# The late residual stream kept by tokens instead of by features

## The chip, the cores and the metric

One NeuronCore of a Trainium2 chip runs the whole program. The metric is device time in microseconds, the median of several executions. The engines are TensorE (PE, with PEld for its weight loads), VectorE (DVE), ScalarE (ACT), GpSimd (POOL) and the DMA queues, of which SyncE (SP) issues the hardware ones.

## The reference, cut to what matters

256 tokens of width D = 1024 pass through two blocks. The first (two layers of attention, pooling and a sparse expert network) is not changed. The second has six residual updates, each of this form, with ALPHA = sqrt(2):

```python
def layer_norm(x, g, b):
    mu = jnp.mean(xf, axis=-1, keepdims=True)
    var = jnp.mean(jnp.square(xf - mu), axis=-1, keepdims=True)
    return ((xf - mu) * lax.rsqrt(var + LN_EPS)).astype(x.dtype) * g + b
...
def post_norm_update(x, y, gate, res_w, g, b):
    return layer_norm(DN_ALPHA * x + res_w * gate * y, g, b)
```

y is the output of a sublayer on `x * (1 + scale) + shift`: a SwiGLU network (1024 to 2 x 2816 to 1024; res_w 0.5), a neighbourhood attention with an output projection, or a three-tap convolution with input and output projections (res_w 1). gate, shift and scale are rows of width D computed from the condition vector. The order of the second block is ffn.0.0, attention (qkv, na_o), ffn.0.1, ffn.1.0, convolution (conv_in, conv_o), ffn.1.1. The five updates behind na_o, ffn.0.1, ffn.1.0, conv_o and ffn.1.1 are called boundaries 0 to 4 here; behind boundary 4 the result is the output.

## The kernel before

Everything streams through one weight stream. SP loads units of 128 x 1024 fp32 (512 KB) into a ring of four `raw` tiles. ACT splits each half of a unit (128 x 512) into a high part `wh` (L677, `hi`), DVE makes the low part `wl` (L1135, `lo`), and PE does three products for each pair of operands (high x high, high x low, low x high). wh and wl are rings of four halves, so ACT and DVE run at most two units ahead of PE, and each half is given back by PE through `halves_free`. The order of instructions on each engine is written out by hand; semaphores join them. Some units are "folds": DVE multiplies 128 x 1024 weights by a condition vector and sums (L1159), which gives one column of the modulation table `mod2`.

The activations lie by features: `X` is 128 partitions (features within a tile) x 8 tiles (k) x 256 tokens. A norm statistic is therefore a sum over partitions, which PE makes with a matrix of 1/D (`column_mean`, L2219), the result being spread over all partitions.

`pairs` is a SwiGLU stage: 22 rounds of two input units (gate and up projection, PE L2032 to L2035, operand stationary weights) and one output unit. The output unit is applied by `token_rows`: tokens are the stationary side, so its sum lies by tokens in banks 0 to 3 (two token tiles x two halves of 512 features). na_o and conv_o are `product` stages instead (PE L2010 to L2012): a unit gives one output feature tile, and DVE adds it to X at once with the gate as a column (`residual`, L1206). One unit needs all eight operand tiles.

What happens at a boundary behind a SwiGLU stage, in order: PE drains (`finish_acc`); ACT and DVE copy the four banks to `token_sums` (L834, L1344); PE turns them by 16 transposes (`turn_sum`, L2210); DVE adds each feature tile to X (`stream_sum`, L1349); PE sums for the mean (L2219); DVE subtracts it (`centre`, L1767); ACT squares (L813); PE sums again (L2219); ACT takes the root (L817); DVE inverts 128 x 256 values (`invert`, L1318); then for each of the eight tiles DVE scales (L1305), ACT writes the high part XH with the shift (L806), DVE the low part XL (L1296), and PE does the first two units of the next stage tile by tile as XH and XL come (`merged_opening`, L2032). Behind na_o and conv_o the order is the same from the mean on.

The residual base of the next boundary, ALPHA * (g * normed + b), is made in X during the next stage: DVE multiplies (`update_view`, L1773), POOL adds the bias column (L659). Behind boundary 4 DVE multiplies by the inverse (L1996), ACT applies g and b (L1112) and SP stores X in four DMAs (L588).

In the conv_in stage DVE also does the convolution (`convolve`, five operations on each tile), and conv_o opens when all eight operand tiles are there. `keep_busy` is PE work without a use, between sums and opening.

Of the kernel before, what the change touches and what calls it, by code (L numbers as in the profile page):

```python
# [113 lines left out]
def plan():  # L114
# [32 lines left out]
    add("na_o", KT, True, KT)  # L147
# [3 lines left out]
    add("conv_o", KT, True, KT)  # L151
# [60 lines left out]

def column_places():
    at, out = 0, {}
    for name, n in COLUMNS:
        out[name] = (at, n)
        at += n
    return out, at
# [37 lines left out]
def build(nc, ctx, stream, columns, tables, x_in, ctx_in, rpb, c_rows, h_spill, c_spill, out):  # L256
# [61 lines left out]
    UNREAD = 62  # L318
    banks = [ctx.enter_context(nc.psum_tensor(f"bank{i}", [P, 512], F32)) for i in range(8)]
# [38 lines left out]
    CONV, CU, CT = 16384, 2048, 4352  # L358

# [26 lines left out]


# [54 lines left out]
    acc_done = sem("acc_done")  # L442
# [29 lines left out]
    view_coef_ready = sem("view_coef_ready")  # L472

# [26 lines left out]


    @block.sync
    def _(sp):
# [82 lines left out]
        for k in range(0, KT, 2):  # L586
            sp.wait_ge(x_done, KT * DEPTH + k + 2)
            sp.dma_start(out[:, k:k + 2, :], X[:, k:k + 2, :]).then_inc(stored, 16)  # L588
        sp.wait_ge(stored, 16 * KT // 2)
# [3 lines left out]
    def _(pool):  # L593
# [60 lines left out]
        for n, name in enumerate(("ffn.0.0.x", "qkv", "ffn.0.1", "ffn.1.0", "conv_in", "ffn.1.1")):  # L654
            pool.wait_ge(xl_ready, made[name])
            pool.wait_ge(view_coef_ready, n + 1)
            for k in range(KT):
                pool.wait_ge(view_step, KT * n + k + 1)
                pool.tensor_scalar(X[:, k, :], X[:, k, :], view_coef[:, 1, k:k + 1], None, ALU.add)\  # L659
                    .then_inc(view_ready, 1)  # L660


    @block.scalar
    def _(act):
# [165 lines left out]
        def copy_sum():  # L830

            act.wait_ge(acc_done, seen("acc_done"))
            for half in range(2):
                act.activation(token_sums[:, 0, HALF * half:HALF * (half + 1)], banks[half][:, :],  # L834
# [10 lines left out]
        for l in range(DEPTH):  # L845
# [139 lines left out]
            if l == 0:  # L985
                copy_sum()
# [16 lines left out]
        def layer_norm(updates, func=ACT.Silu):  # L1003
            seen("stat_ready")
            take_table(ACT.Sqrt)
            squares(X, ZSQ, centred, "centred")
            token_root(banks[7], func, rms, updates)


        hooks = {-1: copy_sum, 0: lambda: squares(X, ZSQ, x_done, "x_done"),  # L1010
# [9 lines left out]
        hooks = {-1: copy_sum, 1: context_squares, 4: lambda: stream_root(banks[7][:, 0:T], 1)}  # L1020
# [16 lines left out]
        copy_sum()  # L1037
# [49 lines left out]
        head_pair_out(KT - 1)  # L1087
        product(stages["na_o"], then=stages["ffn.0.1"], both=True)
        layer_norm(2)
        operand(range(KT), modul, shift)  # L1090
        pairs(stages["ffn.0.1"], 2, ACT.Silu, then=stages["ffn.1.0"], opened=True)
        copy_sum()
        hi(stages["ffn.1.0"], 1)
        layer_norm(3)
        operand(range(KT), modul, shift)
        pairs(stages["ffn.1.0"], 2, ACT.Silu, then=stages["conv_in"], opened=True)
        copy_sum()
        hi(stages["conv_in"], 1)
        layer_norm(4)
        operand(range(KT), modul, shift)  # L1100
        product(stages["conv_in"], to_arena(CONV), then=stages["conv_o"], opened=True)
        operand(range(KT), modul)
        product(stages["conv_o"], then=stages["ffn.1.1"], both=True)
        layer_norm(5)
        operand(range(KT), modul, shift)
        pairs(stages["ffn.1.1"], 2, ACT.Silu, opened=True)
        copy_sum()
        layer_norm(6)

        for k in range(KT):  # L1110
            act.wait_ge(centred, seen("centred"))
            act.activation(X[:, k, :], X[:, k, :], ACT.Identity, bias=column("ln_b.1.2", k),  # L1112
                           scale=column("ln_g.1.2", k)).then_inc(x_done, 1)
# [3 lines left out]
    def _(dve):  # L1117
# [222 lines left out]
        def stream_sum(factor, view, semaphore):  # L1340

            dve.wait_ge(acc_done, seen("acc_done"))
            for half in range(2):
                dve.tensor_copy(token_sums[:, 1, HALF * half:HALF * (half + 1)], banks[2 + half][:, :])\  # L1344
# [34 lines left out]
        for l in range(DEPTH):  # L1379
# [362 lines left out]
            if l == 0:  # L1742
                stream_sum(lambda k: mod1[:, 0, 40 + k:41 + k], X_, x_done)
# [15 lines left out]
        def residual_factor(l, base, side, res):  # L1759
            step(dve.tensor_scalar(scale[:, :], modulation(l, base, 2, side), res, None, MUL))  # L1760
            settle()

# [19 lines left out]
        def last_experts():  # L1782
            stream_sum(lambda k: mod1[:, DEPTH - 1, 40 + k:41 + k], X_, x_done)
# [29 lines left out]
        def context_sum():  # L1813
            stream_sum(factor_of_sum, ctx_tiles, evacuated)
# [27 lines left out]
        stream_sum(factor_of_sum, X_, evacuated)  # L1842
# [4 lines left out]
        product(st, None, 3, 9)  # L1847
# [67 lines left out]
        dve.wait_ge(view_ready, 1 + 2 * KT)  # L1915
        add_bias(0, 2, 40, 48)
        add_bias(0, 2, 48, 72)
        residual_factor(0, 24, 0, 1.0)

        def coefficients(l, which, next_l, next_base):  # L1920

            name = (f"ln_g.{l}.{which}", f"ln_b.{l}.{which}")
            operand_coefficients(next_l, next_base, 0, *name)
            stream_coefficients(*name)

        def layer_norm(then):

            centre(X_)
            lo(then, 1)
            invert(rms)  # L1930
            operand(X_, modul, factor, shift, rms)

        def ffn(name, l, which, updates, then, after=None):

            def coefficients_after():
                if name == "ffn.1.1":
                    add_bias(1, 2, 64, 72)
                residual_factor(l, 0 if which == 0 else 48, 0, 0.5)
                if after is not None:
                    dve.wait_ge(view_ready, 1 + KT * updates)  # L1940
                    add_bias(1, 2, *((0, 24) if after == (1, 0) else (24, 40)))
                    coefficients(l, which, *after)
            hooks = {n + 1: lambda n=n: update_view((2 * n, 2 * n + 1)) for n in range(4)}
            hooks[8] = coefficients_after
# [765 lines left out]
```

## Time and profile before

| | |
|---|---|
| three runs | 3606.43, 3608.0, 3611.11 us; median 3608.0 us |
| profiled execution | span 3608.2 us |
| busy share | PE 97%, PEld 88%, DVE 79%, ACT 57%, POOL 6% |
| mean granted clock of PE | 0.994 of full speed |
| largest groups on DVE and ACT | wl 1453.1 us (2180 x 691 ns), wh 1318.5 us (2180 x 629 ns) |
| DMA | 788.31 MB, mean 218 GB/s |

The span is one execution from first to last instruction; it stands 0.2 us from the median of the runs. A busy PE is one whose pipeline holds something; whether it does useful work must be read from the lines it executes.

### The profile page before, as it was taken

Reading aid. Unit: us, or ns where it says so; the run is one execution under the profiler, and the core shown is the slowest. Engines: PE = TensorE matmul, PEld = TensorE weight load, DVE = VectorE, ACT = ScalarE, POOL = GpSimd, SP = SyncE. Lnnn points to the kernel's source line nnn. Section 1 sums busy time; section 2 is a strip of 40 time slices with the busy share of each in tenths; the row PEclk is TensorE's granted clock in tenths of the full one; section 3 lists DMA queues with packets and bytes.
Section 4 is the critical chain, followed back from the end, with each engine's and each line's share of the span. In section 5 each row is a group of like instructions: output and inputs, shape, how many; then the busy total and the mean of one; then the engine's idle time right before and its main releaser. Section 6 shows DMA issues by size and latency. Waiting matters only on the chain.

```text
span 3608.2 us, 66759 instructions
## 1 busy us (share of the span) xinstructions
PE 3492.3 (97%) x22828; PEld 3162.8 (88%) x22828; DVE 2866.3 (79%) x5956; ACT 2053.0 (57%) x4303; POOL 228.9 (6%) x341
## 2 busy tenths in 40 slices
PE   6999999999999999999999999999999999999998
PEld 6988999998888888999998888898987888889887
DVE  6876987767777778798968778688887788887776
ACT  4554558875555455457875556444454655555555
POOL 0000111110000000111110000010001010101000
PEclk8999999999999999999999999999999999999999
DMA  8556666667776657667757777776766177676463
GB/s 304 199 172 216 223 218 219 220 208 240 241 240 212 224 179 247 225 219 232 245 182 254 240 241 257 220 238 230 251 226 222 54 239 250 199 250 203 146 225 130
DMA packets 246521, 788.31 MB, mean 218 GB/s; under 512 B 30160, under 2 KB 62928, under 8 KB 246048
## 3 DMA queue, kind: packets, MB, share of 16 engines
q1 hardware_dynamic: 230544, 737.78, 63.3%
q0 software_dynamic: 15760, 47.78, 3.7%
q8 instruction: 120, 1.97, 0.2%
q14 instruction: 97, 0.79, 0.1%
HBM read 749.78 MB, written 35.65 MB: 218 GB/s over the span
## 4 chain that ended last, share of the span: by engine, by line
PE 72%; DVE 12%; PEld 7%; issue 4%; DMA 2%; ACT 2%; PEldq 1%; SPq 0%; ACTq 0%; DVEq 0%
PE bank L2010 11%; PE bank L2011 10%; PE bank L2012 10%; PE bank L2032 9%; PE bank L2125 6%; PE bank L2127 6%; PE bank L2126 6%; PE bank L2033 4%; DVE wl L1135 4%; PE bank L2379 3%; PEld bank L2125 2%; PEld bank L2127 2%; PEld bank L2126 2%; DMA raw<-stream 2%; PE bank L2219 2%
## 5 line engine op out<-in xcount | busy, mean ns | idle before, releaser
L1135 DVE TENSOR_TENSOR wl<-raw,wh 128x512 fp32r<-128x512 f32 x2180 | 1453.1, 691 | 462.7 <-ACT wh L677 454.9
L677 ACT ACTIVATE wh<-raw 128x512 fp32r<-128x512 f32 x2180 | 1318.5, 629 | 802.1 <-PE bank L2127 389.9
L2010 PE MATMUL bank<-XHL,wh 128*128 128x256 f32 x3424 | 992.8, 290 | 40.7 <-DVE wl L1135 25.8
L2011 PE MATMUL bank<-XHL,wh 128*128 128x256 f32 x3424 | 970.8, 284 | 0.0
L2012 PE MATMUL bank<-XHL,wl 128*128 128x256 f32 x3424 | 970.6, 283 | 0.0
L2010 PEld LDWEIGHTS bank<-XHL,wh 128*128 128x128 f32 x3424 | 658.3, 192 | 58.7 <-issue 31.8
L2011 PEld LDWEIGHTS bank<-XHL,wh 128*128 128x128 f32 x3424 | 659.1, 192 | 1.8 <-issue 1.0
L2012 PEld LDWEIGHTS bank<-XHL,wl 128*128 128x128 f32 x3424 | 658.3, 192 | 0.0
L2125 PE MATMUL bank<-wh,AH 128*128 128x512 f32 x1464 | 571.6, 390 | 3.7 <-DVE wl L1135 2.1
L2126 PE MATMUL bank<-wl,AH 128*128 128x512 f32 x1464 | 570.1, 389 | 0.0
L2127 PE MATMUL bank<-wh,AL 128*128 128x512 f32 x1464 | 569.6, 389 | 0.0
L2032 PE MATMUL bank<-XHL,wh 128*128 128x512 f32 x1372 | 494.1, 399 | 4.8 <-DVE XHL L1296 4.8
L2033 PE MATMUL bank<-XHL,wl 128*128 128x256 f32 x1372 | 384.9, 281 | 0.0
L2125 PEld LDWEIGHTS bank<-wh,AH 128*128 128x128 f32 x1464 | 275.0, 188 | 60.6 <-issue 2.8
L2127 PEld LDWEIGHTS bank<-wh,AL 128*128 128x128 f32 x1464 | 274.9, 188 | 57.6
L2126 PEld LDWEIGHTS bank<-wl,AH 128*128 128x128 f32 x1464 | 275.1, 188 | 56.2
L2032 PEld LDWEIGHTS bank<-XHL,wh 128*128 128x128 f32 x1372 | 258.1, 188 | 64.4 <-issue 6.7
L2033 PEld LDWEIGHTS bank<-XHL,wl 128*128 128x128 f32 x1372 | 259.2, 189 | 7.6
L959 ACT ACTIVATE side<-bank 128x256 f32<-128x256 f32 x256 | 98.1, 383 | 277.1 <-PE bank L2012 271.2
L631 POOL DMA_DIRECT2D h_spill<-side x256 | 138.4, 541 | 1000.4 <-ACT side L959 988.6
L953 ACT ACTIVATE side<-side,routed 128x128 f32<-128x128 f32 x512 | 163.0, 396 | 0.9
L1693 DVE TENSOR_TENSOR side<-side,arena 128x256 f32<-128x256 f32 x256 | 159.5, 623 | 0.1
(272 smaller groups left out, 4251.5 us busy)
## 6 DMA issues: line engine op xcount, KB each, us to landing
raw<-stream SPq DMA_DIRECT2D x1340, 512.0 KB, 4.4
h_spill<-side POOLq DMA_DIRECT2D x256, 128.0 KB, 3.4
side<-h_spill SPq DMA_DIRECT2D x256, 128.0 KB, 3.8
arena<-rpb POOLq DMA_DIRECT2D x4, 1024.0 KB, 28.9
arena<-tables POOLq DMA_DIRECT2D x2, 832.0 KB, 8.6
X<-x_t POOLq DMA_DIRECT2D x1, 1024.0 KB, 8.2
side<-c_rows POOLq DMA_DIRECT2D x2, 512.0 KB, 7.7
c_spill<-side POOLq DMA_DIRECT2D x2, 512.0 KB, 4.5
```

Of the source, the lines that this page charges most:

```text
L677: act.activation(wh[:, n % 4, :], raw[:, q % 4, HALF * half:HALF * (half + 1)], ACT.Copy).then_inc(hi_ready, 1)
L953: last = act.activation(by_weight[:, b % 2, n * P:(n + 1) * P], unweighted[:, n * P:(n + 1) * P], ACT.Copy, scale=routed[:, 2, t:t + 1])
L1135: tt_op(wl[:, n % 4, :], raw[:, q % 4, HALF * half:HALF * (half + 1)], wh[:, n % 4, :].bitcast(F32), SUB).then_inc(lo_ready, 1)
L1693: tt_op(AP_[:, j % 2, :].unsqueeze(2), HV[:, j % 4, :].unsqueeze(2), gates[:, :, bass.ds(j + more, 1)], MUL).then_inc(gate_done, 1)
L2010: pe.matmul(out, wh[:, n % 4, a:b], moving_h, start=start, stop=False, skip_group_check=check)
L2011: pe.matmul(out, wh[:, n % 4, a:b], moving_l, start=False, stop=False, skip_group_check=check)
L2012: return pe.matmul(out, wl[:, n % 4, a:b], moving_h, start=False, stop=stop, skip_group_check=check)
L2032: pe.matmul(out, wh[:, n % 4, a:b], both, start=kt == 0, stop=False, skip_group_check=True)
L2033: return pe.matmul(out[:, 0:T], wl[:, n % 4, a:b], high, start=False, stop=False, skip_group_check=True)
L2125: pe.matmul(out, high, wh[:, n % 4, :], start=first, stop=False)
L2126: pe.matmul(out, high, wl[:, n % 4, :], start=False, stop=False)
L2127: last = pe.matmul(out, low, wh[:, n % 4, :], start=False, stop=final)
```

## The change

X is read and written by tokens behind na_o (`XT`, the same memory as 128 tokens x 2 token tiles x 1024 features) and is never turned into features again except into the operand. Norm statistics become two columns (one value for each token of a tile), g, b and gate become rows of 1024 spread over all partitions: g and b by a broadcast DMA from a new input `norm_rows`, the gate by a DMA of its column to memory, a broadcast DMA back and a POOL copy that puts it in order. na_o and conv_o take weight rows like the SwiGLU output unit (`projection_rows`), with the unit k needing operand tile k alone. The base is made by POOL alone. The `stream_sum` of earlier stages waits for halves of the last unit instead of a drain. The store goes by tokens.

```diff
 @block.gpsimd
+        def load_gate(n):
+            pool.wait_ge(gate_column, n + 1)
+            pool.dma_start(gate_spill[n, :].rearrange("(p k) -> p k", k=KT), scale[:, :]).then_inc(gate_spilled, 16)
+            pool.wait_ge(gate_spilled, 16 * (n + 1))
+            pool.dma_start(A(GATE_SPREAD, D), gate_spill[n:n + 1, :].broadcast_to([P, D])).then_inc(gate_loaded, 16)
+            pool.wait_ge(gate_loaded, 16 * (n + 1))
+            pool.tensor_copy(A(GATE_ROW, D).rearrange("p (k w) -> p k w", w=P),
+                             A(GATE_SPREAD, D).rearrange("p (w k) -> p k w", k=KT)).then_inc(gate_ready, 1)
...
+        load_gate(0)
+        for n, name in enumerate(("ffn.0.1", "ffn.1.0", "conv_in", "ffn.1.1")):
+            pool.wait_ge(xl_ready, made[name])
+            load_norm(n)
+            pool.wait_ge(norms_loaded, 32 * (n + 1))
+            for tt in range(TT):
+                pool.tensor_tensor(XT[:, tt, :], XT[:, tt, :], A(NORM_ROWS[n], D), ALU.mult).then_inc(base_step, 1)
+            for tt in range(TT):
+                pool.wait_ge(base_step, TT * n + tt + 1)
+                pool.tensor_tensor(XT[:, tt, :], XT[:, tt, :], A(NORM_ROWS[n] + D, D), ALU.add).then_inc(base_ready, 1)
+            load_gate(n + 1)
+        load_norm(4)
 @block.scalar
+        def token_statistics(n):
+            for c in range(len(CHUNKS)):
+                act.wait_ge(local_mean, len(CHUNKS) * n + c + 1)
+                act.activation(A(SQUARED + HALF * c, HALF), tokens_of(c), ACT.Square, bias=stat(LOCAL + c),
+                               accum_out=stat(SPREAD + c)).then_inc(spread_ready, 1)
...
+        def boundary(n, func=ACT.Silu):
+            token_statistics(n)
+            act.wait_ge(inverse_ready, n + 1)
+            for half in range(2):
+                part = XT[:, 0, HALF * half:HALF * (half + 1)]
+                act.activation(part, part, ACT.Identity, bias=stat(OFFSET), scale=stat(INVERSE)).then_inc(normed_first, 1)
+            for k in range(KT):
+                act.wait_ge(moved_ready, KT * n + k + 1)
+                act.activation(XH[:, k, :], modul[:, k, :], ACT.Copy).then_inc(xh_ready, 1)
+            if func is not None:
+                take_table(func)
 @block.vector
+        def token_sums_closed(st, n):
...
+                step(tt_op(A(GATED + HALF * c, HALF), banks[2 * tt + half][:, :], gate_row(half), MUL))
...
+                step(dve.scalar_tensor_tensor(tokens_of(c), base, base_scale, A(GATED + HALF * c, HALF), MUL, ADD,
+                                              accum_out=stat(TOTAL + c)))
...
+            gated(0)
+            gated(1)
+            if n == 0:
+                dve.wait_ge(base_turned, 1)
+            added(0)
+            gated(2)
+            added(1)
+            mean(0)
+            gated(3)
+            added(2)
+            mean(1)
+            added(3)
+            mean(2)
+            mean(3)
...
+        def boundary(st, n, then):
+            token_sums_closed(st, n)
+            lo_half(then, 1, 0)
+            variance(n)
+            lo_half(then, 1, 1)
+            inverse(n)
+            tt_op(stat(OFFSET, 1), stat(MEAN, 1), stat(INVERSE, 1), MUL).then_inc(inverse_ready, 1)
+            for half in range(2):
+                part = XT[:, 1, HALF * half:HALF * (half + 1)]
+                dve.tensor_scalar(part, part, stat(MEAN + 1), stat(INVERSE + 1), ADD, MUL).then_inc(normed_second, 1)
...
+            def moved(k):
...
+                dve.tensor_scalar(modul[:, k, :], turned_tile(n, k), coef[:, 0, k:k + 1], coef[:, 1, k:k + 1], MUL,
+                                  ADD).then_inc(moved_ready, 1)
+            moved(0)
+            for k in range(KT):
+                if k + 1 < KT:
+                    moved(k + 1)
+                dve.wait_ge(moved_ready, KT * n + k + 1)
+                rest((k,), modul)
...
+        co = stages["conv_o"]
+        rest((0, 1), modul)
+        product(co, None, 0, 1)
         convolve(KT - 1)
+        rest((2,), modul)
+        for k in range(3, KT):
+            product(co, None, k - 2, k - 1)
+            rest((k,), modul)
         add_bias(1, 2, 40, 64)
+        gate_factor(1, 24, 1.0, 3)
 @block.tensor
-        def finish_acc():
-            pe.drain().then_inc(acc_done, 1)
+        def boundary(n):
+            pe.wait_ge(local_mean, len(CHUNKS) * n + 1)
+            keep_busy(18, banks[4])
+            for half in range(2):
+                pe.wait_ge(normed_first, 2 * n + half + 1)
+                pe.wait_ge(normed_second, 2 * n + half + 1)
...
+                        last = pe.transpose(turned_tile(n, o)[:, tt * P:(tt + 1) * P], XT[:, tt, o * P:(o + 1) * P],
+                                            ident[:, :])
...
+        projection_rows(stages["na_o"], 0, KT - 1)
...
+        for tt in range(TT):
+            for o in range(KT):
+                last = pe.transpose(banks[4 + 2 * tt + o // 4][:, (o % 4) * P:(o % 4 + 1) * P],
+                                    X[:, o, tt * P:(tt + 1) * P], ident[:, :])
+        last.then_inc(base_turned, 1)
+        projection_rows(stages["na_o"], KT - 1, KT)
+        boundary(0)
```

In `token_sums_closed`, gated(c) multiplies a bank of 128 x 512 by the gate row, added(c) adds it to the base with a running sum, and mean(c) makes the column of a chunk's mean; the four chunks are (tile 0, half 0), (tile 1, half 0), (tile 0, half 1), (tile 1, half 1). `token_rows` and `projection_rows` signal `first_tokens` behind the first token tile of each half of the last unit. Behind boundary 4, DVE does two `scalar_tensor_tensor` of 128 x 512 for each of the four chunks (centre and g; inverse and b), and SP stores each chunk (256 KB). In the SwiGLU stages `update_view` is gone from DVE, and the gate column is made in round 8 of 22; for boundary 3 it is made in conv_o, as shown.

## Rows read from the trace of the kernel before

**Rows 1.** Page, busy time of the engines.

```profile
PE 3492.3 (97%) x22828; PEld 3162.8 (88%) x22828; DVE 2866.3 (79%) x5956; ACT 2053.0 (57%) x4303; POOL 228.9 (6%) x341
```

**Rows 2.** Timeline, boundary 1: start, duration, engine, line, tiles, count [idle before].

```profile
3065.78 2.49 DVE L1135 TENSOR_TENSOR wl<-raw,wh 128x512 fp32r<-128x512 f32 x4
...
3066.61 0.47 PE L2125 MATMUL bank<-wh,AH 128*128 128x512 f32 x1 [0.29 <-DVE wl L1135]
...
3069.23 0.39 PE L2127 MATMUL bank<-wh,AL 128*128 128x512 f32 x1
...
3070.61 1.94 PE L2210 MATMUL bank<-ident,arena 128*128 128x128 f32 x16 [0.99 <-DVE arena L1344]
...
3081.29 1.75 DVE L1318 RECIPROCAL arena<-arena 128x256 f32<-128x256 f32 x1 [1.31 <-ACT arena L817]
...
3084.78 0.47 PE L2032 MATMUL bank<-XHL,wh 128*128 128x512 f32 x1 [0.96 <-DVE XHL L1296]
```

**Rows 3.** Timelines of PE and ACT, boundary 0.

```profile
2872.07 3.62 PE L2219 MATMUL bank<-X,mean_d 128*128 128x256 f32 x16
...
2884.46 0.47 PE L2032 MATMUL bank<-XHL,wh 128*128 128x512 f32 x1 [0.96 <-DVE XHL L1296]
...
2889.11 0.62 ACT L677 ACTIVATE wh<-raw 128x512 fp32r<-128x512 f32 x1
...
2890.63 0.44 PE L2032 MATMUL bank<-XHL,wh 128*128 128x512 f32 x1
```

**Rows 4.** Timeline, conv_o; windows (last: PE's clock, DMA share, GB/s).

```profile
3359.73 2.10 DVE L1294 TENSOR_TENSOR XHL<-arena,XHL 128x256 fp32r<-128x256 f32 x6
...
3389.75 0.48 DVE L1206 SCALAR_TENSOR_TENSOR X<-bank,scale,X 128x256 f32<-128x256 f32 x1 [1.20 <-PE bank L2012]
...
3401.93 0.47 PE L2032 MATMUL bank<-XHL,wh 128*128 128x512 f32 x1 [0.96 <-DVE XHL L1296]
...
3365.00:3370.00 5.00, 3.64 (x18) 3.43 (x18) 3.90 (x13) 1.57 (x4) 0.00 (x0) 0.55 0.28 93
```

**Rows 5.** Timeline of the end.

```profile
3583.31 1.29 DVE L1135 TENSOR_TENSOR wl<-raw,wh 128x512 fp32r<-128x512 f32 x2
...
3601.40 4.04 ACT L1112 ACTIVATE X<-X,cols 128x256 f32<-128x256 f32 x8 [0.77 <-DVE X L1996]
```

**Rows 6.** Groups by form behind 2600 us: busy, mean ns of one.

```profile
L1901 DVE TENSOR_SCALAR arena<-arena,small 128x512 f32<-128x512 f32 x32 | 14.1, 483 | 0.6
...
L1065 ACT ACTIVATE arena<-bank,small 128x512 f32<-128x512 f32 x32 | 21.7, 684 | 6.4 <-DVE small L1891 6.4
...
L821 ACT ACT_TABLE_LOAD x10 | 12.8, 1283 | 0.2
```

**Rows 7.** POOL's operations; DVE without and beside them; windows of ffn.0.1.

```profile
L659 POOL TENSOR_SCALAR X<-X,view_coef x48: 917/1565/1951, 2369.9 to 3449.2; 128x256 f32<-128x256 f32 x48
...
L653 POOL TENSOR_SCALAR arena<-arena 128x2048 f32<-128x2048 f32 x1 | 5.9, 5937 | 10.7 <-DMA arena<-tables 10.7
...
2361.48 2.63 DVE L1135 TENSOR_TENSOR wl<-raw,wh 128x512 fp32r<-128x512 f32 x4
...
2369.98 2.90 DVE L1135 TENSOR_TENSOR wl<-raw,wh 128x512 fp32r<-128x512 f32 x4
...
2900.00:3050.00 150.00, 150.00 (x791) 128.41 (x790) 127.13 (x250) 83.20 (x162) 9.96 (x8) 1.00 0.77 253
```

**Rows 8.** DMA issues (KB, us to landing); a wait in the chain.

```profile
h_spill<-side POOLq DMA_DIRECT2D x256, 128.0 KB, 3.4
...
arena<-rpb POOLq DMA_DIRECT2D x4, 1024.0 KB, 28.9
...
side<-c_rows POOLq DMA_DIRECT2D x2, 512.0 KB, 7.7
...
side<-c_spill POOLq DMA_DIRECT2D x2, 512.0 KB, 4.0
...
2258.63 15.26 DMA raw<-stream
```

More of the change, by code:

```diff
@@ L1036, in _ @@
         product(st, keep, 0, 1)
-        copy_sum()
+        copy_sum(stages["ffn.0.0.x"])
         product(st, keep, 1, 5)
@@ L1087, in _ @@
         head_pair_out(KT - 1)
+        take_table(ACT.Sqrt)
         product(stages["na_o"], then=stages["ffn.0.1"], both=True)
-        layer_norm(2)
-        operand(range(KT), modul, shift)
+        boundary(0)
         pairs(stages["ffn.0.1"], 2, ACT.Silu, then=stages["ffn.1.0"], opened=True)
-        copy_sum()
+        take_table(ACT.Sqrt)
         hi(stages["ffn.1.0"], 1)
-        layer_norm(3)
-        operand(range(KT), modul, shift)
+        boundary(1)
         pairs(stages["ffn.1.0"], 2, ACT.Silu, then=stages["conv_in"], opened=True)
-        copy_sum()
+        take_table(ACT.Sqrt)
         hi(stages["conv_in"], 1)
[L1099 to L1105, printed above, removed]
-        pairs(stages["ffn.1.1"], 2, ACT.Silu, opened=True)
[L1107 to L1113, printed above, removed]
+        boundary(2, None)
+        st = stages["conv_o"]
+        product(stages["conv_in"], to_arena(CONV), then=st, opened=True)
+        operand((0, 1), modul)
+        for k in range(2, KT):
+            product(st, None, k - 2, k - 1)
+            operand((k,), modul)
+        product(st, None, KT - 2, KT, then=stages["ffn.1.1"], both=True)
+        boundary(3)
+        pairs(stages["ffn.1.1"], 2, ACT.Silu, opened=True)
+        take_table(ACT.Sqrt)
+        token_statistics(4)
     @block.vector
@@ L1935, in coefficients_after, with ffn @@
+        def ffn(name, l, which, n, then, after=None):
             def coefficients_after():
@@ L2531, in _ @@
+        projection_rows(stages["na_o"], 0, KT - 1)
+        pe.wait_ge(view_ready, 1 + 2 * KT)
+        pe.wait_ge(xl_ready, made["na_o"])
+        for tt in range(TT):
+            for o in range(KT):
[3 more added lines that the diff above has]
+        projection_rows(stages["na_o"], KT - 1, KT)
+        boundary(0)
         pairs(stages["ffn.0.1"], 2, opened=True)
-        finish_acc()
@@ L2544, in _ @@
+        keep_busy(4, banks[0])
+        projection_rows(stages["conv_o"], 0, KT)
+        keep_busy(8, banks[4])
+        boundary(3)
         pairs(stages["ffn.1.1"], 2, opened=True)
-        finish_acc()
-        turn_sum()
-        stream_norm(evacuated, "evacuated")
 def shape_tables():
```

284 lines of the change are left out of this document (191 added, 93 removed).

## The prediction, written before the changed kernel was run

> **What bounds the kernel now.** The page comes first: PE is busy for 97% of the span [rows 1], so outside the boundaries the time is PE's and a saving on DVE or ACT is worth nothing. A timeline of each boundary comes next, because there PE's busy time is sums, `keep_busy` and waiting, and the order is a chain over DVE, ACT and PE. At boundary 1 the last wl is ready at 3065.78 + 2.49 = 3068.3 (two of these four belong to the next stage), the last matmul starts at 3069.23, and the first matmul of ffn.1.0 at 3084.78 [rows 2]: 15.5 us, boundary 2 alike. At boundary 0 it is 2872.07 to 2884.46, 12.4 us [rows 3]; at boundary 3 3389.75 to 3401.93, 12.2 us [rows 4]; behind the last wl at 3583.31 + 1.29 = 3584.6 the end takes 23.6 us [rows 5]. The reader is to see that five short stretches, some 80 us in all, hold all that this change can give, and that the rest can only be disturbed. Time is therefore summed boundary by boundary, as the shift of the first matmul behind each.
>
> **A boundary behind a SwiGLU stage (1 and 2).** Removed: the drain, copies, adding, two column means, the 1.75 us inversion of 128 x 256 [rows 2]. In their place: DVE can begin at 3068.3, when its wl are done, since the first token tile's bank closes half-way through PE's last six matmuls. A two-input operation of 128 x 512 has a pitch of 2.49 / 4 = 0.62 us [rows 2]; with its running sum 0.70 is taken (an estimate, one short accumulator read more). Four gated, four added, four short means of 0.12: 2.5 + 2.8 + 0.5 = 5.8, to 3074.1. ACT squares two chunks behind the last means, 0.68 each [rows 6]: 3075.5. Then column operations with a wait each (variance 0.2, root 0.3, inverse and offset 0.4) and half a lo in between, 1.3 in all: 3076.8. Normalising 128 x 512 costs DVE 0.48 [rows 6] and ACT about 0.7, which is the longer; first four transposes 0.5 (1.94 / 16 each [rows 2]), hand-overs 0.3, moved 0.35, ACT's copy 0.4, rest 0.35 (2.10 / 6 [rows 4]) and 0.2 to PE: 2.8, to 3079.6. Against 3084.78: **5.2 us**. At boundary 2 a fold of two pitches is behind the normalising, half of it open: **4.6**. Each of these sums is held good to 1.5 us.
>
> One work moves into the open. `take_table(Silu)` was hidden beside the inversion; now it stands behind the last XH, and a table load takes 1.28 us [rows 6]. Queued behind it on ACT is the high part of the third unit. Before, this was at 2889.11, and PE took that unit up at 2890.63, 6.2 us behind the opening's start [rows 3]. After it: opening paced at 0.72 for a tile (moved and rest), XH(7) at +4.45, table to +5.9, hi +6.5, lo +7.1, PE at +7.3. **Loss 1.1 us** at boundaries 0, 1 and 3; at boundary 2 there is no table load, and the faster pace gives 0.3.
>
> **Boundary 0.** Weight rows need 12 matmuls of 512 columns in place of 24 of 256; by the pitch (3069.23 - 3066.61) / 11 = 0.24 [rows 2], 0.23 in an unbroken run, a unit is 2.73 us against 24 x 0.12 = 2.88, 1.2 us for eight. Sixteen transposes for the base are put in front of the last unit, 1.94 us, and the table load before its second hi opens 0.4. The projection so ends 0.8 later, near 2872.9. DVE starts 1.9 before that (at 2871.0), needs 5.8 and then the same 1.4 + 1.3 + 2.8 = 5.5: 2882.3 against 2884.46, **2.1 us**; with the table 1.0.
>
> **Boundary 3.** Before, conv_o's first unit waited for all eight operand tiles, six of which DVE gave from 3359.7 on and two only behind the last convolution, and PE then ran part of it slowly: between 3365 and 3370 the granted clock is 0.55, partly at the 1.2 GHz level [rows 4], behind five microseconds in which PE was half idle. After it, unit 0 starts with tile 0, at 3360.1; each later unit's lo and rest come in time (unit 1 at 3362.8, unit 2 at 3365.6), so the projection ends at 3360.1 + 8 x 2.73 = 3382 against some 3389.6. DVE could start at 3380.5 and PE open at 3391.8, 10 us early. But the gate row is not there. Its column is made behind rest(7), which waits for lo(6), which waits for unit 4: 3360.1 + 5 x 2.73 + hi 0.6 + lo 0.65 + rest 0.35 + two column steps 0.4 = 3375.8, with a wait's play 3375.9. Behind it are a 4 KB write, a broadcast read of 512 KB and a POOL copy of 128 x 1024. The write: nothing so small is shown; 128 KB land in 3.4, so 3.0 is taken (bounds 2.0 and 3.4). The read: 4.0 to 7.7 for 512 KB, 4.6 taken as nearest to those of one DMA alone [rows 8]. The copy: 5.94 / 2 = 3.0 by the large POOL operation, up to 1.95 x 4 = 7.8 by the small ones beside DVE [rows 7], 3.3 taken because DVE waits here. With 0.7 of semaphores: 11.6, so gate at 3387.5, bounds 3385.6 and 3395.5. All of DVE's chain is queued behind that wait, and PE waits for DVE. PE opens at 3387.5 + 5.8 + 5.5 = 3398.8; PE will have been idle some 7 us and its clock may be low, 0.5 more: 3399.3 against 3401.93, **2.6 us**, with the table 1.5; bounds +3.4 and -6.5.
>
> **The end.** First bank closed at 3585.0, DVE 5.9 to 3590.9; columns and squares to 3592.5; three weighted chunks 0.62 each, then inverse and four finished chunks, of which DVE has 2.5 + 0.2 + 2.5 = 5.2 in one run from 3592.0: the last is done at 3597.2. Before, the last was done at 3605.44 [rows 5] and the span ended 2.8 behind. So **8.2 us**.
>
> **Drains.** The first sum (behind the experts of layer 0) has its boundary as in rows 2: transposes start 1.4 behind the start of the last matmul, of which a first half copied early gives back 1.1. Three others have other PE work behind them: 0.5 together. **1.6 us.**
>
> **What is added beside PE.** POOL now does four two-input operations of 128 x 1024 in each of four stages. Alone 3.0 each by one input, 6 to 8 at most beside DVE [rows 7]: 12 to 32 us at the head of stages of 100 us and more (2884.46 to 3084.78 is one with its boundary [rows 2, 3]), early enough. DVE beside POOL went from 2.63 to 2.90 for four wl [rows 7], 10%. DVE is busy 127.1 of 150 us in ffn.0.1 [rows 7]; it loses 3 us of `update_view` (8 x 0.4, the pitch of like operations), and 10 to 30% of 20 us is 2 to 6. Cost taken: **1 us** in all (0 to 6). Norm rows are 1 MB at five places and gates 0.5 MB at five, 7.5 MB beside a stream that already uses 0.77 of the DMA time [rows 7]. When POOL loaded four bias tables of 1 MB and more than 2 MB else, the chain waited 15.3 us for `raw` [rows 8], about 2.3 for each MB. The norm rows come while the ring is full and DMA idle, and the ring covers about 2 us elsewhere: **2 us** (0 to 17). The Trainium skill says in "SBUF — State Buffer", Who interferes with whom, that a DVE instruction with two SBUF inputs contends with a GpSimd instruction that reads SBUF and that the pair of ports is an exclusive lock, whose loser "fully blocks". By the rows above DVE went on at 0.72 a wl during POOL's operations, so the trace does not show a full block; what a full one would make is rival 3.
>
> Sum: 1.0 + (5.2 - 1.1) + (4.6 + 0.3) + 1.5 + 8.2 + 1.6 - 1 - 2 = 18.3. The profiled execution has 3608.2, the median of the runs 3608.0; 3608.2 - 18.3 = 3589.9, and less the 0.2 of the median 3589.7: **3590 us**, taken against the median.
>
> **Rivals.** (1) The gate row of boundary 3 comes at its late bound, 3395.5, and costs 8 more: 3598. For it: a broadcast of one row and a strided copy are shown nowhere. Against: the taken bounds are already of contended operations. (2) The pieces overlap better, or the gate is at its early bound and DMA and POOL cost nothing: 2 + 1 + 2 + 3 for the five chains, 3582. (3) POOL blocks DVE for the whole of its operations, ending slower: 18 us of lock in each of four stages, less 4 of ring (two units) and 15% of idle DVE, is 11 each; 3590 + 44 - 1 = 3633. It decides once the stages lose more than 4.6 us each. For it: the POOL operations are four times longer than any shown beside DVE and read two inputs. Against: the 10% above. (4) The broadcasts cost the stream 2.3 for each of 7.5 MB: 15 more, 3605, no change. Against: most fall where DMA is idle. (5) The removal of the drains gives nothing: 3592, within the forecast's own play.
>
> **Chances.** Forecast 0.53, (1) 0.13, (2) 0.17, (3) 0.07, (4) 0.07, others 0.03, taken as slower. 0.2% of 3608 is 7.2 us, about what a measurement of this kernel tells from no change, so the line is at 3600.8: faster 0.83, same 0.07, slower 0.10. The range takes in (1) and (2) whole, and reaches 3579 to 3603 with 1 us of the bounds' own play at the fast side and the clock's at the other; some 0.83 of the chance lies in it.
>
> **What would show it.** The first matmul of ffn.1.0 should start about 10.4 us behind the last one of ffn.0.1 instead of 15.5. At boundary 3 DVE should wait for POOL's copy for 7 us. ACT's table load should stand between the last XH and the third unit's high part. The rounds of the SwiGLU stages should take as long as before while POOL works; longer rounds speak for rival 3, waits for `raw` for rival 4. Wrong in the sum if the DVE chain of 5.8 is longer, since it counts five times.

## The result and the profile after

The changed kernel takes 3615.79 us, the median of 11 runs (3611.75 to 3620.93), against 3607.41 (3605.09 to 3611.11, 11 runs) for the kernel before on the same chip: a ratio of 1.0021 [1.0014, 1.0029]. The forecast was 3590, from 3579 to 3603. It was wrong, and on the other side. The profiled execution has a span of 3610.7, 2.5 above that of before. Of the 8.4 between the medians these two traces show 2.5. A run's time stands some 1.8 above its span (3612.5 and 3610.7 here); by this the traced execution of before would be one of 3610.0, 2.6 above its median (an estimate), and that of the changed kernel is 3612.5, 3.3 below its own. All times here are of executions in the chip's usual state: one of e3 (7753 us) and one of the kernel before beside it (8760 us) are left out.

The page after, against [rows 1]: PE is busy 20 us less, DVE 17 more, POOL 29 more.

```profile
span 3610.7 us, 66220 instructions
...
PE 3471.9 (96%) x22548; PEld 3137.1 (87%) x22548; DVE 2883.2 (80%) x5952; ACT 2045.6 (57%) x4291; POOL 257.5 (7%) x350
...
arena<-norm_rows POOLq DMA_DIRECT2D x10, 512.0 KB, 5.0
...
arena<-gate_spill POOLq DMA_DIRECT2D x5, 512.0 KB, 5.8
```

PE's timeline at boundary 1, against [rows 2]. The opening starts 3077.51 - 3067.52 = 10.0 us behind the start of the last matmul; it was 15.5.

```profile
3067.52 0.40 PE L2340 MATMUL bank<-wh,AL 128*128 128x512 f32 x1
...
3077.51 0.47 PE L2245 MATMUL bank<-XHL,wh 128*128 128x512 f32 x1 [0.40 <-DVE XHL L1391]
```

So what the change was made of works here. The loss lies behind the opening. PE's waits, by line (total, times, longest): L2245 is PE's line for the SwiGLU input units, L2437 `keep_busy` in the boundary. The first line was not on the list before; the second is boundary 3, where DVE waits for the gate.

```profile
PE bank L2245 <- DVE wl L1232: 15.6, 7, 4.4
...
PE bank L2437 <- DVE small L2061: 9.4, 2, 8.1
```

The timelines of POOL and of DVE in the first rounds of ffn.1.0 (L739 multiplies by g, L742 adds b):

```profile
3083.03 1.05 POOL L730 DMA_DIRECT2D arena<-norm_rows  x2 [108.44 <-DVE XHL L1391]
3088.58 5.65 POOL L739 TENSOR_TENSOR X<-X,arena 128x1024 f32<-128x1024 f32 x2 [4.49 <-DMA arena<-norm_rows]
3094.19 6.10 POOL L742 TENSOR_TENSOR X<-X,arena 128x1024 f32<-128x1024 f32 x2
```

```profile
3086.15 1.28 DVE L1232 TENSOR_TENSOR wl<-raw,wh 128x512 fp32r<-128x512 f32 x2
...
3088.47 3.48 DVE L1232 TENSOR_TENSOR wl<-raw,wh 128x512 fp32r<-128x512 f32 x2
3091.88 3.42 DVE L1256 SCALAR_TENSOR_TENSOR raw<-raw,side 128x1024 f32<-128x1024 f32 x1
3095.24 0.08 DVE L1256 DVE_READ_ACCUMULATOR raw<-raw,side 128x1 f32 x1
3095.24 5.60 DVE L1232 TENSOR_TENSOR wl<-raw,wh 128x512 fp32r<-128x512 f32 x2
```

Before POOL starts, two wl take 1.28. The first wl of the next pair starts before POOL and takes its usual 0.68 (two follow each other at 0.62). From there, while POOL's four operations run (3088.58 to 3100.29), DVE gets through a wl, a fold and two wl: one operation for each of POOL's, at 2.8 to 2.9 for a wl in place of 0.62 and 3.42 for the fold in place of 1.2. Each ends 0.5 to 1.1 us behind the end of one of POOL's (3091.96 behind 3091.41, 3095.30 behind 3094.22), that is by about its own length: DVE is not slowed, it is held until POOL's operation is over and then runs. POOL waits in its turn: its operation behind the fold takes 3.32, the one before it 2.84. The columns count a held DVE as busy, which is why the hold shows nowhere as a wait of DVE.

In a table by steps, as shifts of PE's timeline between these two traces (us; minus is earlier than before; how far the first step is to be trusted comes further down):

| step | forecast | measured |
|---|---|---|
| up to the end of attention (drains) | -1.6 | -6.6 |
| boundary 0, without what is behind its opening | -2.1 | -2.2 |
| boundary 1 | -5.2 | -5.6 |
| boundary 2 | -4.6 | -5.2 |
| boundary 3 | -2.6 | -1.2 |
| the end | -8.2 | -8.2 |
| behind the four openings: table load and pace 3.0, POOL 1, DMA 2 | +6.0 | +31.5 (7.1, 8.3, 7.2, 8.9) |
| sum | -18.3 | +2.5 |

The chain of waits through boundary 3 (start, duration, what), against [rows 4], and then that of the end, against [rows 5]:

```profile
3379.35 3.66 DMA gate_spill<-scale
3383.01 0.29 issue
3383.30 6.47 DMA arena<-gate_spill
3389.77 0.05 issue
3389.82 2.02 POOL arena L724
3391.84 0.02 issue
3391.86 1.29 DVE arena L2046 x2
...
3395.09 6.42 PE bank L2437 x36
```

```profile
3595.92 1.29 DVE arena L2046 x2
...
3604.46 1.41 DVE X L2197 x2
```

### The profile page after: what moved, and what is told of

Same layout as the page of the kernel before. It is cut to its first block, busy times and chain, and to the rows that moved or that the text cites. A ratio compares the mean times of both kernels' runs of the same rounds, so it can differ in the third digit from the quotient of the medians.

```text
span 3610.7 us, 66220 instructions
## 1 busy us (share of the span) xinstructions
PE 3471.9 (96%) x22548; PEld 3137.1 (87%) x22548; DVE 2883.2 (80%) x5952; ACT 2045.6 (57%) x4291; POOL 257.5 (7%) x350
## 4 chain that ended last, share of the span: by engine, by line
PE 80%; DVE 14%; DMA 2%; ACT 2%; issue 1%; POOL 0%; DVEq 0%; SPq 0%; ACTq 0%
PE bank L2223 10%; PE bank L2224 10%; PE bank L2225 10%; PE bank L2338 9%; PE bank L2339 9%; PE bank L2340 9%; PE bank L2245 8%; DVE wl L1232 5%; PE bank L2246 4%; PE bank L2591 3%; DMA raw<-stream 2%; PE bank L2248 1%; DVE raw L1256 1%; ACT wh L761 1%; PE bank L2575 1%
## 5 line engine op out<-in xcount | busy, mean ns | idle before, releaser
L1232 DVE TENSOR_TENSOR wl<-raw,wh 128x512 fp32r<-128x512 f32 x2172 | 1471.1, 701 | 482.4 <-ACT wh L761 473.9
L2223 PE MATMUL bank<-XHL,wh 128*128 128x256 f32 x3296 | 956.1, 290 | 36.1 <-DVE wl L1232 25.0
L2224 PE MATMUL bank<-XHL,wh 128*128 128x256 f32 x3296 | 934.5, 284 | 0.0
L2225 PE MATMUL bank<-XHL,wl 128*128 128x256 f32 x3296 | 934.4, 283 | 0.0
L2223 PEld LDWEIGHTS bank<-XHL,wh 128*128 128x128 f32 x3296 | 633.6, 192 | 53.1 <-issue 25.8
L2224 PEld LDWEIGHTS bank<-XHL,wh 128*128 128x128 f32 x3296 | 634.6, 193 | 1.8 <-issue 1.0
L2225 PEld LDWEIGHTS bank<-XHL,wl 128*128 128x128 f32 x3296 | 633.6, 192 | 0.0
L2245 PE MATMUL bank<-XHL,wh 128*128 128x512 f32 x1372 | 500.6, 403 | 18.8 <-DVE wl L1232 15.6
L2246 PE MATMUL bank<-XHL,wl 128*128 128x256 f32 x1372 | 387.4, 282 | 0.0
L2245 PEld LDWEIGHTS bank<-XHL,wh 128*128 128x128 f32 x1372 | 260.7, 190 | 82.7 <-DVE wl L1232 14.8
L2246 PEld LDWEIGHTS bank<-XHL,wl 128*128 128x128 f32 x1372 | 261.9, 191 | 7.4
L1256 DVE SCALAR_TENSOR_TENSOR raw<-raw,side 128x1024 f32<-128x1024 f32 x123 | 159.3, 1295 | 0.9 <-DMA raw<-stream 0.9
```

Source lines behind the costliest of these rows:

```text
L1232: tt_op(wl[:, n % 4, :], raw[:, q % 4, HALF * half:HALF * (half + 1)], wh[:, n % 4, :].bitcast(F32), SUB).then_inc(lo_ready, 1)
L1256: dve.scalar_tensor_tensor(unit, unit, 1.0, c, MUL, MUL, accum_out=dst).then_inc(folded, 1)
L2223: pe.matmul(out, wh[:, n % 4, a:b], moving_h, start=start, stop=False, skip_group_check=check)
L2224: pe.matmul(out, wh[:, n % 4, a:b], moving_l, start=False, stop=False, skip_group_check=check)
L2225: return pe.matmul(out, wl[:, n % 4, a:b], moving_h, start=False, stop=stop, skip_group_check=check)
L2245: pe.matmul(out, wh[:, n % 4, a:b], both, start=kt == 0, stop=False, skip_group_check=True)
```

## The experiments

The question was what takes the 31.5 us behind the openings. Four causes were open: POOL's two-input operations hold DVE (rival 3); the norm rows' DMAs cost the stream (rival 4); the table load that now stands in the open on ACT; and, at boundary 3, the gate row. All kernels are edits of the changed one, except the last. Each was timed in turns with the kernel before.

**e1: POOL's base left out.**

```diff
-            for tt in range(TT):
-                pool.tensor_tensor(XT[:, tt, :], XT[:, tt, :], A(NORM_ROWS[n], D), ALU.mult).then_inc(base_step, 1)
...
+            pool.sem_inc(base_ready, TT)
```

> Leaves out the base of boundaries 1 to 4 (GpSimd signals at once; the norm rows are still loaded), so the output is another one. Theory L (GpSimd's two-input operations of 128 x 1024 hold up DVE's two-input ones): the four stretches behind an opening give back 5.5 to 7 us each, 22 to 28 in all; a span near 3585. Theory D (the stretches are slow because 1 MB of norm rows is loaded beside the stream): no change, near 3611. Theory T (only the table load is in the way there): no change either.

3587.91 us (3586.97 to 3588.13), ratio 0.994 [0.9924, 0.9957]: 27.9 below the changed kernel, 24.8 in the traces. The window of 25 us at the head of ffn.1.0, first of the changed kernel, then of e1 (start and end, length, then PE, PEld, DVE, ACT, POOL busy with their counts; then PE's granted clock, DMA share, GB/s):

```profile
3085.00:3110.00 25.00, 20.53 (x95) 17.04 (x96) 24.09 (x31) 10.94 (x23) 11.71 (x4) 0.86 0.61 202
```

```profile
3085.00:3110.00 25.00, 25.00 (x133) 21.41 (x133) 21.06 (x41) 13.94 (x27) 0.00 (x0) 1.00 0.80 270
```

With POOL at work DVE is busy for 24.1 of 25 us and does 31 operations; without it, 41 in 21.1. PE loses 4.5 us of busy time and, as it stops and starts, part of its clock (0.86), so it does 95 matmuls instead of 133. The DMA share falls because the ring is not emptied, not because it is full. Behind the openings e1 still loses 4.6 of the 31.5 (1.4, 1.8, 0.0, 1.4), so some 27 belong to POOL's operations, but e1 doesn't say whether by reading two inputs, by their length or by their mere traffic. The 4.6 stand at the three SwiGLU stages, where PE waits three times for the third unit, behind the table load:

```profile
PE bank L2241 <- DVE wl L1228: 3.9, 3, 1.3
```

**e2: the same four operations with one input** (the base is then not g and b; the length is the same).

```diff
-                pool.tensor_tensor(XT[:, tt, :], XT[:, tt, :], A(NORM_ROWS[n], D), ALU.mult).then_inc(base_step, 1)
+                pool.tensor_scalar(XT[:, tt, :], XT[:, tt, :], ALPHA, None, ALU.mult).then_inc(base_step, 1)
...
-                pool.tensor_tensor(XT[:, tt, :], XT[:, tt, :], A(NORM_ROWS[n] + D, D), ALU.add).then_inc(base_ready, 1)
+                pool.tensor_scalar(XT[:, tt, :], XT[:, tt, :], 1.0, None, ALU.mult).then_inc(base_ready, 1)
```

> The four GpSimd operations of a stage take one input of 128 x 1024 instead of two (scaled by a constant, so the base lacks g and b and the output is another one). Theory L1 (the second input makes the block): DVE's wl beside them takes 0.7 us as beside the small one-input operations before, the openings give back 5 us each, a span near 3590. Theory L2 (the length of one operation makes it, whatever the inputs): wl still takes 2.9 us, a span near 3611 or above, since one-input operations take 3.0 alone. Theory D: near 3611 with wl at 0.7.

3588.19 us (3586.8 to 3590.2), ratio 0.9942 [0.9926, 0.9959], the same as without any. Timelines of POOL and DVE in e2, the same place:

```profile
3085.60 6.33 POOL L739 TENSOR_SCALAR X<-X 128x1024 f32<-128x1024 f32 x2 [4.56 <-DMA arena<-norm_rows]
3092.01 6.39 POOL L742 TENSOR_SCALAR X<-X 128x1024 f32<-128x1024 f32 x2
```

```profile
3085.41 2.13 DVE L1232 TENSOR_TENSOR wl<-raw,wh 128x512 fp32r<-128x512 f32 x2
3087.46 1.21 DVE L1256 SCALAR_TENSOR_TENSOR raw<-raw,side 128x1024 f32<-128x1024 f32 x1
...
3088.61 2.13 DVE L1232 TENSOR_TENSOR wl<-raw,wh 128x512 fp32r<-128x512 f32 x2
...
3091.32 1.27 DVE L1232 TENSOR_TENSOR wl<-raw,wh 128x512 fp32r<-128x512 f32 x2
```

POOL works longer (3.2 an operation), yet DVE loses 0.85 once at the start of each, and then goes on at 0.62 a wl and 1.2 a fold. So at this size neither the length nor the traffic is the cause: it is the two-input form. Whether the second input itself or the other instruction (tensor_tensor in place of tensor_scalar) makes it, no run tells apart. A one-input operation is not free either. The trace of before has a longer one, L653 of 128 x 2048 [rows 7], from 2259.63 for 5.94 us, and beside it one wl is held for some 2.9 us:

```profile
2260.74 3.63 DVE L1135 TENSOR_TENSOR wl<-raw,wh 128x512 fp32r<-128x512 f32 x1 [0.42 <-ACT wh L677]
```

**e5: the norm rows loaded twice**, which doubles rival 4's cost (5 MB more).

```diff
-            for which in range(2):
-                pool.dma_start(...)
+            for again in range(2):
+                for which in range(2):
+                    pool.dma_start(...)
+                if not again:
+                    pool.wait_ge(norms_loaded, 64 * n + 32)
```

> Each pair of norm rows is loaded twice, one pair behind the other, 5 MB more in all. Theory D: 2.3 us for each MB that is not hidden, 5 to 9 us slower than the changed kernel. Theory L: GpSimd's operations only start 5 us later in each stage, within 2 us of the changed kernel.

3616.23 us (3614.13 to 3621.39), ratio 1.0024 [1.0015, 1.0034], the changed kernel's own time within the intervals, which leave some 3 us open. The 5 to 9 us of theory D are not there.

**e6: the gate column of boundary 3 made in conv_in**, behind its unit 12.

```diff
         product(st, None, 0, 12, opened=True)
+        add_bias(1, 2, 40, 48)
+        gate_factor(1, 24, 1.0, 3)
...
-        add_bias(1, 2, 40, 64)
-        gate_factor(1, 24, 1.0, 3)
+        add_bias(1, 2, 48, 64)
```

> The gate column of boundary 3 is made in conv_in behind unit 12 (its folds are done by then) instead of in conv_o behind the last operand tile. If the wait for GpSimd's copy is all that holds boundary 3, PE opens ffn.1.1 some 6 to 9 us earlier: a span near 3603 against 3610.7. If something else is late at the same time (DVE's chain, the clock), less than 4 us.

3606.35 us (3604.29 to 3615.0), ratio 0.9994 [0.9985, 1.0004], 9.4 below the changed kernel. POOL's copy and DVE's first gated chunks in e6:

```profile
3336.82 2.15 POOL L724 COPY arena<-arena 128x1024 f32<-128x1024 f32 x1 [6.26 <-DMA arena<-gate_spill]
```

```profile
3387.69 1.28 DVE L2046 TENSOR_TENSOR arena<-bank,arena 128x512 f32<-128x512 f32 x2
```

The row is there 49 us early. PE opens ffn.1.1 10.0 us behind the start of conv_o's last matmul:

```profile
3388.71 0.40 PE L2745 MATMUL bank<-wh,XHL 128*128 128x512 f32 x1
...
3398.71 0.47 PE L2246 MATMUL bank<-XHL,wh 128*128 128x512 f32 x1 [0.40 <-DVE XHL L1391]
```

The changed kernel needs 18.9 there (3384.79 to 3403.65), so the wait for the gate costs 8.9. conv_o itself took 23.3 us in e6 against 21.7, at a granted clock of 0.76 between 3363 and 3370, so 7.3 of it are left over both.

**e3: POOL's operations in 16 pieces of 128x256, back to back; e4: one piece in each round.** POOL waits for DVE's wl of a round before each piece in e4; the work is the same.

```diff
-            for tt in range(TT):
-                pool.tensor_tensor(XT[:, tt, :], ...)
...
+            for piece in range(16):
+                pool.wait_ge(lo_ready, ...)        # e4 alone: the round of this piece
+                part = XT[:, tt, 256 * quarter:256 * (quarter + 1)]
+                pool.tensor_tensor(part, part, A(NORM_ROWS[n] + D * second + 256 * quarter, 256), ...)
```

> GpSimd makes the base in 16 operations of 128 x 256 in a stage instead of 4 of 128 x 1024, one behind the other as before. Theory L (each two-input operation of GpSimd holds DVE's next two-input one until it has ended): DVE takes turns with pieces of 0.6 to 0.7 us instead of 2.9, so it loses about the same 9 us in all but over some 20 us, of which its own idle time covers 3 to 4: 10 to 16 us faster than the changed kernel, a span near 3598. Rival L3 (what counts is the sum of GpSimd's time only): within 3 us of the changed kernel.

> The same 16 pieces, each of which waits for the weights of its own round (one piece for each SwiGLU round, one for each unit in conv_in). Theory L: a round of 8.4 us then has one hold of 0.6 us, less than DVE's idle time there, and nothing is lost: 22 to 28 us faster than the changed kernel, a span near 3586, as without any base. L3: as e3.

e3: 3598.49 us (3595.09 to 3601.49, six runs), ratio 0.9968 [0.9956, 0.9981]. e4: 3588.67 (3587.77 to 3591.38), ratio 0.9943 [0.9926, 0.9961]. In e3 (POOL, then DVE) the pieces run for 18.6 us, and two wl take 1.8 to 2.4 in place of 1.28:

```profile
3091.27 18.59 POOL L743 TENSOR_TENSOR X<-X,arena 128x256 f32<-128x256 f32 x16 [4.63 <-DMA arena<-norm_rows]
```

```profile
3091.03 1.83 DVE L1234 TENSOR_TENSOR wl<-raw,wh 128x512 fp32r<-128x512 f32 x2
3092.79 1.76 DVE L1258 SCALAR_TENSOR_TENSOR raw<-raw,side 128x1024 f32<-128x1024 f32 x1
...
3094.48 2.36 DVE L1234 TENSOR_TENSOR wl<-raw,wh 128x512 fp32r<-128x512 f32 x2
3096.77 0.41 DVE L1328 TENSOR_TENSOR side<-bank,side 128x256 f32<-128x256 f32 x1
...
3100.17 0.71 DVE L1349 CAST AH<-side 128x256 fp32r<-128x256 f32 x1
```

A hold now lasts one short piece, and DVE gets a turn behind each; 17.3 of the 27.9 come back. The last two lines show which operations of DVE are held. One with an input from PSUM (`bank`) beside one from SBUF is not: 0.41, as ever. A cast with a single input, from SBUF, is: 0.71 in place of 0.29. So on DVE's side it need not be two inputs from SBUF. In e4, where a piece comes once a round, DVE loses 0.5 of its slack in a round (two wl in 1.81). PE's waits for wl on the line of the SwiGLU input units (its L2248) are three, short ones, the same three as in e1:

```profile
3105.29 1.81 DVE L1235 TENSOR_TENSOR wl<-raw,wh 128x512 fp32r<-128x512 f32 x2
```

```profile
PE bank L2248 <- DVE wl L1235: 3.9, 3, 1.3
```

All of the loss is given back, with the same two-input work on POOL. What it costs depends on whether the rings of two units can absorb the hold.

**e8: the base on DVE**, eight operations of 128x512, one in a round.

```diff
+        def make_base(n, i):
+            if i == 0:
+                dve.wait_ge(norms_loaded, 32 * (n + 1))
+            c, second = i % 4, i // 4
...
+            tt, half = CHUNKS[c]
+            step(tt_op(tokens_of(c), tokens_of(c), norm_row(n, second, half), ADD if second else MUL))
...
+            hooks = {i + 1: lambda i=i: make_base(n - 1, i) for i in range(8)}
```

> DVE makes the base itself, eight two-input operations of 128 x 512 in a stage, one in each of the rounds 1 to 8 (in conv_in one for each of the units 3 to 10); GpSimd only loads the rows. Theory L: 0.62 us for each round fits into DVE's idle time, so as fast as e4, a span near 3586. If DVE has no room left, 8 x 0.6 x 4 = 19 us of the gain are lost: 3605.

3587.58 us (3586.42 to 3591.2), ratio 0.9941 [0.9923, 0.9959]. 8 x 0.69 of open DVE work in a stage cost as little as POOL's pieces in e4: DVE has that slack in each round, but not 9 us of it at once.

**e7: the Silu table loaded by the first Silu**, not in the boundary.

```diff
-        def boundary(n, func=ACT.Silu):
+        def boundary(n, func=None):
```

> The Silu table is loaded by the first Silu of the stage instead of behind the last high part of a boundary (boundaries 0, 1 and 3). Theory T: PE's wait of 1.3 us for the third unit at each of the three openings goes, and in the changed kernel GpSimd's block would take some of it back: 1 to 4 us faster. Rival: the load lands between second parts and Silu, PE waits there instead, no change.

3613.93 us (3607.13 to 3621.78), ratio 1.0014 [1.0004, 1.0024], 1.9 below the changed kernel, with intervals that overlap. ACT's timelines of the changed kernel and of e7: the load has moved behind the third unit's high part, into round 0.

```profile
3082.22 1.28 ACT L905 ACT_TABLE_LOAD   x1
3083.52 0.20 ACT L905 ACTIVATE small<-eps 128x1 f32<-128x1 f32 x1
3083.63 1.13 ACT L761 ACTIVATE wh<-raw 128x512 fp32r<-128x512 f32 x2
```

```profile
3087.77 1.28 ACT L846 ACT_TABLE_LOAD   x1
```

**e9: e4, e6 and e7 together. e11: e4 and e6 together. e10: e8, e6 and e7 together.** Their edits are those above.

> e4 (pieces spread over the rounds), e6 (early gate column) and e7 (late table load) together. If the three losses are apart from each other: 28 + 9 + 2 to 4 less than the changed kernel, 3575 to 3579.

> e4 and e6 without e7: 3578 to 3581. Against e9 it shows what the table load costs once GpSimd's block is gone: Theory T 1.3 us at three openings, 4 us; rival: DVE's ring takes it up within the first round, under 1 us.

> e8 (base on DVE, one operation for each round), e6 and e7 together: within 2 us of e9.

e9: 3583.34 us (3580.64 to 3584.74), ratio 0.9926 [0.991, 0.9943]. e11: 3583.45 (3581.34 to 3585.85), 0.9931 [0.9914, 0.9947]. e10: 3579.61 (3578.35 to 3580.06), 0.9917 [0.9901, 0.9934], the fastest here; the kernel before took 3609.63 beside it, 30.0 more. The medians of e9 and e11 are the same, 4 to 8 us above what was expected of e9 and 2.5 above what was expected of e11, and e10 is not within 2 us of e9. The traces say where the time lies better than four runs can. In this table "behind openings" is what the stages ffn.0.1, ffn.1.0, conv_in and ffn.1.1 took from the first to the last matmul, less the 625.7 of before (31.4 for the changed kernel, where the steps above, with slightly other ends, have 31.5); "boundary 3" goes from conv_in's last matmul to the first of ffn.1.1; the last column is where attention ends, up to which all these kernels but before are the same.

| trace | behind openings | boundary 3 | end of attention | span |
|---|---|---|---|---|
| before | 0 | 45.5 | 2846.5 | 3608.2 |
| after | 31.4 | 44.3 | 2839.9 | 3610.7 |
| e1 | 4.6 | 43.8 | 2842.4 | 3585.9 |
| e2 | 4.4 | 44.3 | 2842.4 | 3586.2 |
| e3 | 14.1 | 44.0 | 2845.1 | 3598.3 |
| e4 | 4.4 | 42.8 | 2843.3 | 3585.7 |
| e6 | 30.6 | 37.0 | 2840.7 | 3603.5 |
| e8 | 5.1 | 45.2 | 2839.1 | 3584.6 |
| e9 | 5.1 | 37.0 | 2845.5 | 3582.7 |
| e10 | 2.8 | 37.0 | 2843.2 | 3578.3 |
| e11 | 6.9 | 35.4 | 2842.4 | 3579.9 |

Where POOL's holds are gone, moving the table load gives 1.9 (e9 against e11) and 2.3 (e10 against e8) behind the openings; e9's waits for wl on the line of the SwiGLU input units fall from e11's 3.9 in three to

```profile
PE bank L2249 <- DVE wl L1235: 1.5, 2, 0.9
```

In the medians of e9 and e11 it can't be seen: attention ends 3.1 us later in e9's trace, and its boundary 3 is 1.6 longer, by conv_o. The early gate gives 7.3 at boundary 3 behind e4, but conv_in takes 2.5 longer in e9 and e11 (73.8 against 71.3): PE waits there for wl five times, 2.9 us in all, where it waits three times, 0.9, in e4. Hence a gain of 5.2 in the medians and not e6's 9.4. With the base on DVE conv_in stays as it was (72.1 in e8 and e10), which is 1.7 of the 3.7 between e10 and e9; another 2.2 are the end of attention. The same window as above, in e10:

```profile
3085.00:3110.00 25.00, 25.00 (x132) 21.18 (x131) 22.61 (x46) 14.49 (x29) 0.00 (x0) 1.00 0.83 286
```

**e12: the kernel before, with POOL's bias as a second input.** Was it the form, or what the change does around it?

```diff
-                pool.tensor_scalar(X[:, k, :], X[:, k, :], view_coef[:, 1, k:k + 1], None, ALU.add)\
+                pool.tensor_tensor(X[:, k, :], X[:, k, :], view_coef[:, 1, k:k + 1].broadcast_to([P, T]), ALU.add)\
```

> The kernel before with one edit: GpSimd adds the bias column as a second input of 128 x 256 that repeats it, in place of a column operand (48 operations, the same result). Theory L (the second input alone makes the block): the wl beside them take 1.2 us and more instead of 0.72 in this kernel too; the median stays within 3 us of before, since two such holds fit into a round. Rival (it was the length of the operations or their rows in the arena): wl as in the kernel before.

3611.14 us (3608.62 to 3615.0), ratio 1.0004 [0.9994, 1.0013], no change. POOL and DVE in e12, a piece of ffn.1.0:

```profile
3108.00 1.72 POOL L659 TENSOR_TENSOR X<-X,view_coef 128x256 f32<-128x256 f32 x2 [173.53 <-DVE X L1773]
```

```profile
3108.14 2.13 DVE L1135 TENSOR_TENSOR wl<-raw,wh 128x512 fp32r<-128x512 f32 x2
```

Beside it two wl take 2.13, where beside the one-input form they take 0.72 each [rows 7]. So the hold can be had in the kernel before as well, by one edit (1.07 a wl, a little less than the 1.2 expected); in pieces of 0.9 it costs nothing there.

## Why the prediction was wrong

**The step that failed** is "What is added beside PE": "Cost taken: 1 us in all (0 to 6)". It measured DVE's loss beside POOL by operations with one input [rows 7], 2.63 to 2.90, and used it as a rate, 10 to 30%, for operations with two. What the runs showed in its place is no rate: a two-input operation of POOL holds DVE's next operation that takes all its inputs from SBUF (wl, fold, and in e3 a cast) until it ends. Four times 3 us back to back are 11.7 us in which DVE does four operations (about 3.1 us of work). 8.6 are lost; a part is covered by the rings, the rest is PE's. By the stages of the changed kernel less those of e1 it is 5.6, 6.5, 7.1 and 7.6, some 27 in all, against the 1 us taken. That is rival 3, which had 0.07. It took 18 us of POOL work and reached 11 a stage; POOL needed only 12, hence 6 to 8. My argument against it, the 10% in rows 7, was from the other form. The prediction also takes L653 [rows 7] for an operation alone, and rival 3 says that no such long one was shown beside DVE; the wl of 3.63 above stood beside it, in the trace of before, and was overlooked. The sentence on the Trainium skill ("SBUF — State Buffer", Who interferes with whom) pointed the right way: its exclusive lock is what the changed kernel's rows show, with 2.8 for a wl in place of 0.62. The trace agrees for two-input operations of POOL; beside one-input operations of POOL, which read SBUF as well, e2 shows one hold of 0.85 and none for the remaining 2.4.

**The chains of the boundaries** were right. 5.6 and 5.2 us against 5.2 and 4.6; boundary 0 2.2 against 2.1, though its sum leaves out the 0.4 that it names for the table load (-1.2 + 1.94 + 0.4 is 1.1, not 0.8); the end 8.2 as forecast, with its DVE run of the columns and sums at 3601.2 - 3595.9 = 5.3 against 5.9.

**Boundary 3**: 1.2 against 2.6. conv_o without its late start takes 3363.1 to 3385.0, 21.9 us, as forecast (3360.1 to 3382), at a granted clock of 1; in most traces of the experiments it took 1.6 more, as in e6. From column to row: write 3.7 (3.0 taken), read 6.5 (4.6 taken, 7.7 the bound), copy 2.0 (3.3 taken): 12.8 against 11.6 in all. The row came at 3391.8, not 3387.5, mostly because conv_o began 3.0 late from the loss before. DVE waited 8.0, as the text said it would (7). The wait is avoidable: e6.

**Rival 4** falls: e5 loads the norm rows twice and is at most some 3 us slower, where the rival asks for 2.3 for each MB. **The table load and the pace** were taken at 3.0 and **the DMA** at 2; e1, which has both and no base on POOL, loses 4.6. Some 2 of it are the table load's (e9, e10), against 3.3 taken; the rest isn't told apart.

**The end of attention** (the drains and what stands before): 6.6 earlier against 1.6. Here the traces differ by themselves. The changed kernel and its eleven edits have the same code up to this point, and attention ends between 2839.1 and 2845.5, at 2842.3 in the mean; the kernel before has 2846.5, e12 2849.0. So the gain is some 5.5, with 3 of play to each side, and more than the 1.6 forecast. At the first sum's transposes it is 1.3 in the mean, where 1.1 was forecast. What the rest is was not tested; this is left open.

Without the base on POOL the forecast would have held: e1 takes 3587.9 against 3590. That is in part luck, since attention ends earlier than forecast and boundary 3 gave less.

**The medians.** The changed kernel, e5, e6 and e7 scatter over 7 to 15 us in 10 or 11 runs, the kernel before over 6 to 7.5 in 11 to 19, e12 over 6, e3 over 6 in six, and the others over 1 to 5 in four runs each. The widest have POOL's long two-input operations. The play up to the end of attention is in all of them. That the hold falls on more or less of DVE's work from run to run would fit the rest, but was not tested.

## What to carry to other kernels

Price work on GpSimd by what DVE must do in the same microseconds, not by its own slack: with two inputs on GpSimd it is also the time of every DVE operation that takes all its inputs from SBUF, and the length of one operation decides, since a ring hides a hold only up to its depth. Give it one input where the result allows it, or cut it in pieces and put one in each round, or leave it on DVE, if DVE has the slack; any of them turned a loss of 0.2% into a gain of 0.6%. A value that takes two DMAs and a copy belongs a stage ahead of its use, as soon as its inputs are there.

## What the hardware showed

- Two-input GpSimd operation of 128x1024 beside two-input DVE operations: a wl takes 2.8 in place of 0.62 us, a fold 3.42 in place of 1.2, each running when GpSimd's has ended. Beside pieces of 128x256 a DVE cast with one input from SBUF takes 0.71 in place of 0.29; a DVE operation with one input from PSUM and one from SBUF keeps its 0.41. DVE's records show it as busy (24.1 of 25 us), never as waiting. Of the rows shown, an excess of a group's mean over its mean elsewhere is the only sign.
- One-input GpSimd operation of the same size, 3.2 us: one hold of 0.85, at its start. One of 128x2048, 5.94 us: a wl of 3.63 beside it.
- GpSimd was faster with two inputs than with one and a constant: 128x1024 in 2.9 against 3.2 (means of 16), though the first shared its time with DVE.
- PE's granted clock fell to 0.86 of full speed over 25 us in which waits for wl broke up its work, a part of what a hold costs.
